# Convolution input projection: seven block products in place of eight, on three token superblocks

## The reference, cut to what matters

```python
h = rms_norm(x, g_pre)
b_gate, c_gate, u_in, z = jnp.split(h @ w_in, 4, axis=-1)      # 2056 x 1024 @ 1024 x 4096
u = c_gate * u_in
up = jnp.concatenate([past.astype(u.dtype), u], axis=1)
y = b_gate * causal_short_conv(up, w_conv, T)                  # three taps along the tokens
out = (y * jax.nn.silu(z)) @ w_out
```

## Time and profile before

| | |
|---|---|
| runs | 2868.95, 2869.64, 2869.67 us; median 2869.64 |
| the profiled execution, first to last instruction (span) | 2864.1 us |
| the same beside the median of the runs | 5.5 us less |
| this phase: first and last product start | 29.8 and 769.2 us |
| TensorE busy over the span | 95% |

### The profile page before, as it was taken

How to read it: one execution, slowest core, us unless ns; L and a number is a source line. 1 busy time by engine, 2 the same in 40 slices (tenths; PEclk the granted TensorE clock), 3 DMA queues, 4 the chain that set the end, 5 groups by cost and what they waited for, 6 DMA issues and landing times. The chain is left out here.

```text
span 2864.1 us, 39445 instructions
## 1 busy us (share of the span) xinstructions
PE 2717.9 (95%) x14124; PEld 2351.9 (82%) x14124; DVE 1189.8 (42%) x2209; ACT 973.7 (34%) x2163; POOL 449.0 (16%) x330
## 2 busy tenths in 40 slices
PE   6999999999799799999989999989999987899997
PEld 5999999999777568888858888877888867788884
DVE  7311111111243355555564554554444433455552
ACT  6211111111155434444443443343333333233332
POOL 1010110101012211111111111111111110233331
PEclk9999999999999999999999999999999985999999
DMA  4232323322455431111131111131111116433330
GB/s 155 85 103 70 109 95 106 103 70 95 142 189 174 139 130 49 41 40 41 63 104 43 48 48 41 46 120 51 60 59 59 50 37 210 170 133 133 134 119 31
DMA packets 128411, 264.49 MB, mean 92 GB/s; under 512 B 14125, under 2 KB 81541, under 8 KB 126794
## 3 DMA queue, kind: packets, MB, share of 16 engines
q1 hardware_dynamic: 122138, 219.41, 23.3%
q10 hardware_dynamic: 6192, 44.01, 4.8%
HBM read 198.21 MB, written 109.19 MB: 107 GB/s over the span
## 5 line engine op out<-in xcount | busy, mean ns | idle before, releaser
L1070 PE MATMUL g_proj<-g_w_hi,g_ht_hi 128*128 128x512 f32 (+1 forms) x1224 | 509.2, 416 | 19.7 <-DVE g_w_lo L1385 19.4
L1072 PE MATMUL g_proj<-g_w_hi,g_ht_lo 128*128 128x512 f32 (+1 forms) x1224 | 485.5, 397 | 0.0
L1071 PE MATMUL g_proj<-g_w_lo,g_ht_hi 128*128 128x512 f32 (+1 forms) x1224 | 485.1, 396 | 0.0
L249 PE MATMUL a_pair<-a_ht_hi,a_w_hi 128*128 128x412 f32 (+1 forms) x1280 | 448.9, 351 | 2.0 <-DVE a_ht_lo L409 2.0
L251 PE MATMUL a_pair<-a_ht_hi,a_w_lo 128*128 128x412 f32 (+1 forms) x1280 | 448.1, 350 | 0.0
L250 PE MATMUL a_pair<-a_ht_lo,a_w_hi 128*128 128x412 f32 (+1 forms) x1280 | 448.0, 350 | 0.0
L1070 PEld LDWEIGHTS g_proj<-g_w_hi,g_ht_hi 128*128 128x128 f32 (+1 forms) x1224 | 223.5, 183 | 72.9 <-DVE g_w_lo L1385 14.2
L1072 PEld LDWEIGHTS g_proj<-g_w_hi,g_ht_lo 128*128 128x128 f32 (+1 forms) x1224 | 223.1, 182 | 64.1 <-issue 3.2
L1071 PEld LDWEIGHTS g_proj<-g_w_lo,g_ht_hi 128*128 128x128 f32 (+1 forms) x1224 | 224.1, 183 | 49.5 <-issue 2.4
L249 PEld LDWEIGHTS a_pair<-a_ht_hi,a_w_hi 128*128 128x128 f32 x1280 | 241.6, 189 | 3.0 <-DVE a_ht_lo L409 2.4
L250 PEld LDWEIGHTS a_pair<-a_ht_lo,a_w_hi 128*128 128x128 f32 x1280 | 241.4, 189 | 1.0
(11 more groups left out here) (222 smaller groups left out, 4924.6 us busy)
## 6 DMA issues: line engine op xcount, KB each, us to landing
out_cache_kv_g_sample<-cache_kv_g ACTq DMA_DIRECT2D x72, 410.0 KB, 3.5
scratch_partial<-g_part SPq DMA_DIRECT2D x48, 520.0 KB, 2.9
d_part<-scratch_partial SPq DMA_DIRECT2D x48, 520.0 KB, 4.6
g_tok<-scratch_hn_rows SPq DMA_DIRECT2D x48, 512.0 KB
a_w_raw<-a_w_in SPq DMA_DIRECT2D x32, 512.0 KB, 5.4
a_x<-x_prompt SPq DMA_DIRECT2D x16, 512.0 KB, 3.5
b_y_raw<-scratch_y_t SPq DMA_DIRECT2D x16, 512.0 KB, 4.3
b_x<-x_prompt SPq DMA_DIRECT2D x16, 512.0 KB
```

Of the source, the lines that this page charges most:

```text
L249: nc.tensor.matmul(out, hi, ht_hi[:, k, cols], start=(k == 0), stop=False)
L1070: nc.tensor.matmul(out, hi, w_hi[:, k, cols], start=(k == 0), stop=False)
L1071: nc.tensor.matmul(out, hi, w_lo[:, k, cols], start=False, stop=False)
L1072: last = nc.tensor.matmul(out, lo, w_hi[:, k, cols], start=False, stop=(k == KT - 1))
```

## The change

It replaces the phase. The 2056 tokens are cut into three superblocks of 688, 688 and 680, each of two halves c (344, 344 or 340). In a superblock, a feature tile's two gates (C and U, or B and Z) by two contraction halves k, against two contraction halves by two token halves, are a 2 x 2 block product, done with seven block products (Strassen, in Winograd's form) in place of eight. One such step is a *quad* q: 3 superblocks x 8 feature tiles x 2 gate pairs = 48 quads. Each has seven terms j, and a term is 4 contraction tiles x 3 matmuls of 344 (340) columns.

- Token blocks and their sums: four blocks and three sums per superblock (VectorE's `token_sum`, 1376 elements a partition), each of the seven split into `x_hi` (ScalarE) and `x_lo` (VectorE's `tokens_lo`, 1376 elements). There is one set of them, rewritten for the next superblock during the last quad of the one before.
- Weights: `load_w(q + 2)` fetches 1 MB for every quad, so `w_in` is read three times in all. VectorE makes four sums of 512 elements (`weight_sums`, one of them over a raw block), ScalarE rounds seven blocks of 512, GpSimd makes seven low halves of 512 (`weights_lo`). `w_hi[j]` and `w_lo[j]` are single: they are rewritten for quad q + 1 when term j of quad q is done.
- Results: terms 4 to 6 add into banks of terms 0, 2 and 3 that ScalarE has copied out before. `u_sum`, `c12` and `c21` are VectorE's, `p57` and `c22` GpSimd's (`corner`). `left` (VectorE) and `right` (GpSimd) make u or y for one half each; taps are 688 wide; `gate_left` and `gate_right` finish y.
- Rows: two buffers `x_buf` in place of three. The first superblock's six tiles are transposed before its first product. Each tile of the later two is loaded twice, once for the squares and once for the transposes, which stand inside quads after term 4; 12 quads have such a tile.
- The cache moves go from ScalarE's queue to SP's, behind `load_w(q + 2)`. VectorE starts with `weight_sums(0, range(4))`, ahead of the memset of `eps`, for which ScalarE's first square now waits.

```diff
-    CHUNK = 412
...
-    GATES = (1, 2, 0, 3)
...
+    HALF = (344, 344, 340)
...
+    GATES = ((1, 2), (0, 3))
+    TERMS = 7
+    A11, S2, S1, S3, A12, S4, A22 = range(TERMS)
+    ROLE = (0, 1, 2, 3, 0, 2, 3)
+    BANKS = ((0, 1, 2, 3), (4, 5, 1, 2))
...
+            def load_w(q):
+                _s, i, kind = place(q)
+                if q >= 2:
+                    sp.wait_ge(s_wlo, terms(q - 2, TERMS - 1))
+                for x, g in enumerate(GATES[kind]):
+                    sp.dma_start(w_raw[q % 2][:, x, :, :], w_view[:, :, g, i * P:(i + 1) * P])\
+                      .then_inc(s_wraw[q % 2], 16)
...
+            for q in range(QUADS):
+                if q + 2 < QUADS:
+                    load_w(q + 2)
+                if q >= 2 and q % 2 == 0:
+                    store_y(q - 1)
+                if q in SQUARE_AT:
+                    load_x(*SQUARE_AT[q], False)
+                if q + 1 in TILE_AT:
+                    load_x(*TILE_AT[q + 1], True)
+                move_caches(q)
...
+            def weights_lo(q, j):
+                if q >= QUADS:
+                    return
+                pool.wait_ge(s_whi, terms(q, j))
+                nc.gpsimd.tensor_tensor(w_lo[j][:], w_source(q, j), w_hi[j][:].bitcast(F32),
+                                        ALU.subtract).then_inc(s_wlo, 1)
+            def corner(q):
+                n = HALF[place(q)[0]]
+                pool.wait_ge(s_copied, 3 * q + 3)
+                nc.gpsimd.tensor_tensor(p57[:, 0:n], p5_sb[:, 0:n], p7_sb[:, 0:n], ALU.add).then_inc(s_p57, 1)
+                pool.wait_ge(s_p57, q + 1)
+                pool.wait_ge(s_usum, q + 1)
+                nc.gpsimd.tensor_tensor(c22[:, 0:n], p57[:, 0:n], u_sum[:, 0:n], ALU.add).then_inc(s_c22, 1)
...
-            def split_w_lo(i, k):
-                pool.wait_ge(s_whi, 4 * i + k + 1)
-                nc.gpsimd.tensor_tensor(w_lo[k][:], w_raw[k % 2][:], w_hi[k][:].bitcast(F32),
-                                        ALU.subtract).then_inc(s_wlo, 1)
-            for k in range(4):
-                split_w_lo(0, k)
-            with pool.Fori(1, NF) as i:
-                for k in range(4):
-                    split_w_lo(i, k)
+            for j in range(TERMS):
+                weights_lo(0, j)
+            for q in range(QUADS):
+                for j in range(4):
+                    weights_lo(q + 1, j)
+                    if j == 0 and q >= 2 and q % 2 == 0:
+                        gate_right(q - 1)
+                corner(q)
+                weights_lo(q + 1, 4)
+                right(q)
+                for j in range(5, TERMS):
+                    weights_lo(q + 1, j)
...
+            def bank_free(q, j):
+                odd = q % 2
+                if j == 0 and q >= 2:
+                    pe.wait_ge(s_left, q - 1)
+                elif j == 1 and q >= 2:
+                    pe.wait_ge(s_usum if odd else s_c12, q - 1 if odd else q)
+                elif j == 2 and q >= 1:
+                    pe.wait_ge(s_usum if odd else s_c21, q)
+                elif j == 3 and q >= 1:
+                    pe.wait_ge(s_c12 if odd else s_c21, q if odd else q - 1)
+                elif j >= 4:
+                    pe.wait_ge(s_copied, 3 * q + j - 3)
...
+            def term(q, j):
+                s = place(q)[0]
+                n = HALF[s]
+                if q % PER == 0:
+                    pe.wait_ge(s_xlo, TERMS * s + j + 1)
+                pe.wait_ge(s_wlo, terms(q, j))
+                bank_free(q, j)
+                out = bank(q, j)[:, 0:n]
+                first, more = j < 4, j >= 4
+                for k in range(HK):
+                    hi, lo = w_hi[j][:, k, :], w_lo[j][:, k, :]
+                    nc.tensor.matmul(out, hi, x_hi[j][:, k, 0:n], start=first and k == 0, stop=False,
+                                     skip_group_check=more)
+                    nc.tensor.matmul(out, hi, x_lo[j][:, k, 0:n], start=False, stop=False, skip_group_check=more)
+                    last = nc.tensor.matmul(out, lo, x_hi[j][:, k, 0:n], start=False, stop=k == HK - 1,
+                                            skip_group_check=more)
+                last.then_inc(s_prod, 1)
...
+            def weight_sums(q, which):
+                if q >= QUADS:
                     return
+                raw, (s1, s2, s4) = w_raw[q % 2], (x[:] for x in w_sum[q % 2])
+                a11, a12 = raw[:, 0, 0:HK, :], raw[:, 0, HK:KT, :]
+                a21, a22 = raw[:, 1, 0:HK, :], raw[:, 1, HK:KT, :]
+                for x in which:
+                    if x == 0:
+                        dve.wait_ge(s_wraw[q % 2], 32 * (q // 2 + 1))
+                        if q >= 2:
+                            dve.wait_ge(s_wlo, terms(q - 2, TERMS - 1))
+                    else:
+                        dve.wait_ge(s_wsum, 4 * q + x)
+                    out, one, two, op = ((s1, a21, a22, ALU.add), (s2, s1, a11, ALU.subtract),
+                                         (a21, a11, a21, ALU.subtract), (s4, a12, s2, ALU.subtract))[x]
+                    nc.vector.tensor_tensor(out, one, two, op).then_inc(s_wsum, 1)
...
+                for j in range(TERMS):
+                    if j == 1:
+                        sum_u(q)
+                    elif j == 2 and q >= 1:
+                        if kind == 1:
+                            taps(q - 1)
+                        else:
+                            gate_left(q - 1)
+                    elif j == 3:
+                        if q in ROOT_AT:
+                            norm_steps(ROOT_AT[q], slice(0, XTILES))
+                        if q in TILE_AT:
+                            normalise(*TILE_AT[q])
+                    elif j == 4:
+                        for x in range(2):
+                            if (q, x) in SUMS_AT:
+                                token_sum(*SUMS_AT[q, x])
+                        if kind == 1:
+                            left(q)
+                    elif j == 5:
+                        sum_c12(q)
+                    elif j == 6:
+                        sum_c21(q)
+                        if kind == 0:
+                            left(q)
+                    if j in (4, 6):
+                        weight_sums(q + 2, (0, 1) if j == 4 else (2, 3))
+                    if last:
+                        tokens_lo(s + 1, j)
```

More of the change, by code:

```diff
@@ new lines, in conv_projection_phase @@
+        y_buf = sb("y", [P, 2 * NMAX])
+        p1_sb, p5_sb, p7_sb, u_sum, p57 = (sb(n, [P, NMAX]) for n in ("p1", "p5", "p7", "u_sum", "p57"))
+        c12, c21, c22 = (sb(n, [P, NMAX]) for n in ("c12", "c21", "c22"))
+        rows, state_rows = t_sum[0], t_sum[1]
+        quad_ps = [ctx.enter_context(nc.psum_tensor(f"a_quad{b}", [P, BANK], F32)) for b in range(6)]
+        tps = [ctx.enter_context(nc.psum_tensor(f"a_tps{b}", [P, BANK], F32)) for b in range(2)]
+        s_gain = sem("gain_landed")
@@ new lines, in conv_projection_phase @@
+        s_rows = sem("rows_landed")
+        s_ident = sem("ident_ready")
+        s_x = [sem(f"x_landed{b}") for b in range(2)]
+        s_eps = sem("eps_ready")
+        s_sumsq = sem("sumsq")
+        s_root = sem("root")
+        s_rstd = sem("rstd_steps")
+        s_xn = sem("x_normalised")
+        s_tr = sem("transposed")
+        s_tr_free = sem("transpose_evacuated")
+        s_t = sem("token_sums")
+        s_xhi = sem("x_hi_ready")
+        s_xlo = sem("x_lo_ready")
+        s_wraw = [sem(f"w_landed{b}") for b in range(2)]
@@ L142, in conv_projection_phase, with place, bank, terms @@
-        STATE_JOB = 1 + 2 * (NT + 1)
+        def place(q):
+            return q // PER, q % PER // 2, q % 2
+        def bank(q, j):
+            return quad_ps[BANKS[q % 2][ROLE[j]]]
+        def terms(q, j):
+            return TERMS * q + j + 1
+        def x_tile(s, j):
+            return XTILES * s + j
+        def x_load(s, j, final):
+            return j if s == 0 else XTILES * (2 * s - 1 + final) + j
+        TWICE = [x_load(SUPS - 1, XTILES - 1, final) for final in range(2)]
+        def x_landed(s, j, final):
+            load = x_load(s, j, final)
+            return 16 * (load // 2 + 1 + len([x for x in TWICE if x <= load and x % 2 == load % 2]))
@@ new lines, in move_caches @@
+            def move_caches(part):
+                for cache, moved in zip(caches, caches_out):
+                    count = cache.shape[1] - 1
+                    pieces = 6 if count >= 1024 else 1
+                    b, piece = part // 6, part % 6
+                    if piece >= pieces:
+                        continue
+                    each = -(-count // pieces)
+                    begin = piece * each
+                    each = min(each, count - begin)
+                    sp.dma_start(moved[b:b + 1, begin:begin + each, :],
+                                 cache[b:b + 1, begin + 1:begin + 1 + each, :]).then_inc(s_moved, 16)
@@ new lines, in gates @@
+            def gates(q):
+                n = HALF[place(q)[0]]
```

(10 more changed lines are left out.)

703 lines of the change are left out of this document (383 added, 320 removed).

## The result

| kernel | median us (lowest to highest) | ratio to before, 95% interval |
|---|---|---|
| before | 2869.3 (2866.0 to 2869.7) | 1 |
| after | 2898.7 (2892.8 to 2900.2) | 1.0104 [1.009, 1.0117] |

The change makes the kernel 29.4 us, 1.0%, slower. Forecast were 2935 us, 65.5 slower, in a range of 2865 to 3010: the direction and the range held, the size was more than twice what came.

The account below looks back on a forecast made before the run. TensorE bounds the convolution phase before; after it, the port shared by VectorE and GpSimd. Quad 0's end 71 + 714 for 47 quads + 50 = 835 us, 65.5 later than 769.5: 2869.6 + 65.5 = 2935 us, range 2865 to 3010.

Parts of the forecast that it names:

- TensorE's pace: Convolution quads: 84 matmuls of 344 columns at 0.1567 us take 13.16 us a quad, 632 us in all instead of 715.
- The exclusion: Convolution quads: VectorE instructions with two SBUF operands and GpSimd's exclude each other, so 3.96 and 12.2 us add to 16.2.
- what would show it: Signs in the convolution phase: stretched weight sums and low halves, GpSimd above 80%, TensorE below 90%, last product near 835 us.
- The hand-over: Convolution quads: fixed parts overlap when the port changes sides, 0.31 us for both sides, taking 1.7 us off 16.2.
- the port's total: Convolution quads: GpSimd's and VectorE's two-SBUF-operand work added, less overlap at hand-overs: 14.5 us a quad.
- 14.5 + 0.24 + 0.5 = 15.2: Convolution quads: port work plus GpSimd's waits before c22 (0.24) and for c12 (0.5), in us a quad; bounds 14.5 and 16.2.
- Start: Convolution start: weight sums and paired token tiles delay the first product to near 54 us; quad 0 ends about 71.
- The extras: Convolution phase: other port work, 15.4 us scalings, 12.7 token sums and 22.3 token low halves at two superblock borders: 50 us.
- The 5.5 us: Whole kernel before: the median run, 2869.6 us, exceeds the profiled span of 2864.1; this difference is kept in the forecast.
- Rival 1: Convolution quads: exclusions fall into idle time, a quad takes 13.16 us, total 2824 us, 1.6% faster; chance 0.12.
- Rival 2: Convolution quads: the weight-load loop binds, landings of 8 us or more give 17 us a quad, 3020 us; chance 0.10.
- Rival 3: Convolution quads, half and half: VectorE's sums fall into GpSimd's waits, 13.4 to 14.3 us a quad, 2851 to 2893; chance 0.08.

Follow-up runs that it names:

- e1: Against after: each VectorE weight sum replaced by a one-operand reduction of the same 512 elements, additions left out (y not the reference's); 2837.4 us.
- e3: Against after: all seven low halves of the weights moved from GpSimd to VectorE; 2827.2 us, 0.9864 of before.
- e10: Against after: all four weight sums of quad q+2 moved behind c12, c21 and left of quad q; 2916.3 us, 1.0163 of before.
- e8: Against after: low half of term 4 moved to VectorE, and quad q+2's weight sums behind c12, c21 and left of quad q; 2902.4 us.
- e6: Against after: one of a quad's seven low halves (term 4) moved from GpSimd to VectorE, behind c12; 2881.0 us, 1.0042 of before.
- e7: Against after: two of a quad's seven low halves (terms 3 and 4) moved from GpSimd to VectorE, behind c12; 2872.0 us, 1.0013 of before.

## Why the prediction was right or wrong, point by point

- **TensorE's pace.** 13.16 us a quad were forecast by a line through two shapes; the odd quads of after run at 13.3 with 344 columns, and e1 and e3 at 13.1 with 340. In the last superblock TensorE loses 1.4 us a quad to waits and to the lower clock; 2 were forecast.
- **The exclusion.** Right, and it is the cause of the loss: e1, which takes only the sums out of it, is 61 us faster than after and 1.0% faster than before. A weight sum averages 1115 to 1458 ns, a low half 1597, and GpSimd is above 80%, as "what would show it" asked; TensorE, at 90 to 93% in the three windows, misses its sign of below 90%. The rival left by e1 alone, that shorter sums only bring c12 forward, falls with e10.
- **The hand-over.** Right: the port's total of 14.5 us stands against 14.51. GpSimd's busy time is 192.85/195 x 14.51 = 14.35 a quad. The Trainium skill, SBUF — State Buffer, section "Who interferes with whom", read literally, gave 16.2; the trace is 1.7 below it, as two neighbours overlap by some 0.3 us (1.70 us for the pair above, not 1.98). One moved low half bears it out (e8, 13.58).
- **The step that failed:** "so I add 0.5 for it and take 14.5 + 0.24 + 0.5 = 15.2". The two waits were put on top of a total that they hardly touch. Between p57 and c22 lie 0.07 us, not 0.24, and GpSimd waits for c12 only 1.0 us in the last 195. Idle time on GpSimd is 14.51 - 14.35 = 0.16 us a quad, not 0.74. The 0.7 us too much, 47 times, is 33 us: the last product was forecast at 835 and ends at 802.5. Once GpSimd is not full, as in e6 and e7, the waits for c12 do count.
- **Start.** First product forecast near 54, measured 53.8; end of quad 0 forecast 71, measured 69.8. The first match is in part luck: tile 0 is transposed from 19.6 us, not 21.6, and quad 1's weight sums, stretched by low halves, then take 5.7 us (43.40 to 49.14) where four free ones take 2.8.
- **The extras.** Forecast 50 us; what is left of the phase is 732.7 - 47 x 14.51 = 51, with 732.7 from 69.8 to 802.45. The quads at a border take 24.4 and 24.3 us, 10 over the others (11 forecast). That the rest agrees is luck: the 12 quads with token tiles are 27 us longer together than at 14.51, where their scalings were put at 15.4, and the token sums, put at 12.7, stand in quads 12, 13, 28 and 29, where quads 12 to 15 and 28 to 31 take 14.57 us. What else lengthens the quads with tiles is open.
- **The tail.** Taken as equal. From the last product's end to the end of the span lie 2088.5 us; 2089 to 2099 in the experiments, and 2094.2 before, where the last product ends at 769.9. So the two profiled executions differ by 26.9 us, 32.6 up to the last product and 5.7 less behind it; the medians differ by 29.4. The rest of the kernel was not touched; where the 5.7 us come from is open, and executions of one kernel differ as much. The 5.5 us that the prediction keeps outside the span are not all outside it: a run's time is about 2 us above its span in the executions of before beside the experiments, so the profiled one was also some 3.5 us quicker than the median. It stands on both sides and changes no forecast.
- **Rival 1** (the port does not bind, 2824) falls for the kernel as forecast, by 14.51 us a quad and by e1; e3, whose low halves have left GpSimd, runs at the pace that it names and comes to 2827. One of its terms was too large: a tile's eight transposes take 1.03 us in e3 (at 164.27) where TensorE does not wait before them, not 2, and most quads that hold a tile take 14.1 there, 0.8 over the 13.3 of the others. **Rival 2** (the load loop, 17 us a quad) falls by e10, and its landings of 8 us or more do not occur: 3.8 to 5.8 us in after. **Rival 3** (13.4 to 14.3 a quad) does not describe after, but holds the pace of e6 and e7. The condition that I gave for level, 13.8 a quad, is close to e7: 13.94 at the end, 2872.

## What to carry to other kernels

Before work is put on GpSimd beside VectorE, add up both engines' instructions that read two SBUF operands, less 0.3 us for each turn, and compare the sum with the engine that is to gain; do not add waits on top of an engine that this total already fills. A 512-element subtraction takes 0.69 us on VectorE and 1.29 on GpSimd, so the engine that looks busier can be the better place. When a queue near its limit is reordered, follow what moves back in every stage: the sums moved behind c12 helped the last superblock where GpSimd had lost a low half, and cost more where token tiles are prepared.

## What the runs showed of the hardware that I had not expected

VectorE's very small instructions are blocked too, even with one tensor operand: the copy of 128x2 above takes 1249 ns (162 for such a copy before), and a scaling of 8 elements 1257 in the last superblock of after (226 before), while e1's one-operand reduction of 512 elements keeps its 682 ns beside a GpSimd at 95%. The same section of the Trainium skill says that copies and `tensor_scalar` can take the shared ports and that `tensor_reduce` never contends on this chip; both rows agree.

TensorE's granted clock fell to the lower level after a stall. In after it had rested 2.40 us for c12 before 602.36; the windows ahead, within and behind:

```profile
597.00:602.00 5.00, 2.96 (x19) 2.68 (x18) 4.37 (x7) 1.60 (x3) 4.92 (x5) 1.00 0.82 288
602.60:605.90 3.30, 3.30 (x13) 3.30 (x13) 3.03 (x3) 0.86 (x2) 3.30 (x3) 0.50 0.03 5
606.00:610.60 4.60, 4.60 (x31) 4.60 (x31) 1.12 (x2) 2.44 (x5) 4.60 (x5) 1.00 0.14 38
```

For 3.3 us it ran at 1.2 GHz, with starts of products 0.28 us apart instead of 0.156, so this stall cost TensorE some 1.5 us (12 x 0.127) more than its own length. It is not every stall's price: of the five waits for c12 of 2.3 to 3.0 us in the last superblock, four are followed by such a stretch, and the one before 747.71 is not. Whether it adds to the pace there, with GpSimd full, no run tells.
